# Feature products of the first block: head and tail of the tokens in one 512-column product, its two halves added by ScalarE and VectorE

## The chip, the cores and the metric

The kernel runs on one core of a Trainium2 chip. The metric is the device time of one execution in microseconds (us), all times below are of this kind.

## The reference

A first block of two layers on 256 tokens of 2048 features, then a second block (modulated norm, banded attention, a two-level mixture of 32 experts). The change is in the first block. Cut to it:

```python
for l in range(DEPTH):                                   # DEPTH = 2
    h = _rms_norm(x, norm_g[l])
    proj = jnp.einsum('bsd,dn->bsn', h, w_in[l])         # 2048 x about 7000
    (a_q, a_k, a_v, a_f, a_gate, b_cq, b_ckv, b_krope, b_gate,
     c_q, c_k, c_v, c_gate) = jnp.split(proj, IN_OFFSETS, axis=-1)
    ...
    a_out = _fox_attention(a_q, a_k, a_v, cum_logf) * silu(a_gate)        # 6 heads
    ...
    b_out = _mla_attention(q_nope, q_rope, k_nope, k_rope, b_v) * silu(b_gate)   # 6 heads
    ...
    c_out = _rms_norm(_diff_attention(...), diff_subln_g[l]) * ... * silu(c_gate)  # 4 heads
    x = x + jnp.einsum('bsm,md->bsd', concat(a_out, b_out, c_out), w_out[l])
```

## The kernel before

All products in fp32 are made of fp32r parts: each operand is split into a head (rounded) and a tail (what is left), and a product is head x head + head x tail + tail x head, three matmuls that add up in one bank of PSUM. The helper `three` issues them (L1022 to L1024).

The weights of the first block come as 73 pieces per layer, 128 partitions x 2048 numbers each, in the order of `layer_schedule`: 16 token pieces and one feature piece kr, then for each of six A heads the feature pieces aq, ak, ag (query, key, gate), four low-rank pieces, six gates bg, for each of four C heads cq, ck, cg, and 16 output pieces. SyncE's queue loads pieces, and in between 64 ada pieces per layer (weights for the second block), into a ring `raw` of five. ScalarE writes a piece's head into `w_head` in two halves (L834), VectorE its tail into `w_tail` (L1232); both rings have three slots. At step g the two engines split piece g + 2. A feature piece on TensorE is 16 steps of k (2048 features by 128), with the weights as the stationary operand and 256 tokens as the moving one; the result, 128 features x 256 tokens, fills half a bank. One of four banks is taken in turn. TensorE adds one to `full`, and VectorE brings the bank out times `rrow`, the tokens' inverse norms: L1308 for q (with the scale), L1311 for k, and L1326 for a gate, which then is bounded below in L1327. It then adds one to `free`.

All engines follow one list of steps, `all_steps`, each in its own order of instructions. Between the pieces stand the steps of the heads, sorted by `in_turn`: first score, then gated, then gate, then turn, value and others, then ada, soft. In a score TensorE multiplies q by k (L1171; A adds the decay in L1176), VectorE adds the mask and takes the maximum (L1423 to L1431, "shifted"), ScalarE takes the exponentials (L984, L986). In gate VectorE does L1326 and L1327 into the single buffer `gate_raw`, ScalarE then the sigmoid (L955 to L957), and in gated (L1334), a piece later, VectorE multiplies the two. In soft VectorE scales the probabilities (L1437 to L1440), which TensorE transposes in turn (L1184) after the next piece. In value TensorE multiplies by v (L1193, L1195), and VectorE brings this out (L1469, for C L1462 and the square L1464, whose sum over features TensorE makes in L1201). In ada VectorE multiplies an ada piece and sums it (L1347). L1485 and L1013 split the mixed heads for the output pieces.

The second block has semaphores, tallies and a list of its own and starts when the first is done.

Of the kernel before, what the change touches and what calls it, by code (L numbers as in the profile page):

```python
# [21 lines left out]
F32R = mybir.dt.float32r  # L22
I32 = mybir.dt.int32
ALU = mybir.AluOpType
# [33 lines left out]
class Tally:  # L58

    def __init__(self):
        self.order = {}

    def add(self, sem, event, it=0):
        table = self.order.setdefault(sem, {})
        assert (event, it) not in table, (sem, event, it)
        table[event, it] = len(table) + 1

    def at(self, sem, event, it=0, each=1):  # L70

# [410 lines left out]
def first_block(nc, whole, ctx, d, x, ssq_x, ssq_g, c0, mod):  # L482
# [40 lines left out]
    for l, s in flat:  # L523
        kind = s[0]
        if kind == "squares":
            for t in range(TT):
                tally.add("squared", (s[1], t), l)
            if s[1] == 3 and l < DEPTH:
                tally.add("rstd", "x", l)
        elif kind == "gained":  # L530
            for t in range(TT):
                tally.add("gained", (s[1], t), l)
                tally.add("squared", ("gained", s[1], t), l)
        elif kind == "x_diag":
            tally.add("diag", "x", l)
        elif kind == "split_x":
            tally.add("h_head", s[1], l)
            tally.add("h_tail", s[1], l)
        elif kind == "low_stats":
            tally.add("rstd", "low", l)  # L540
            tally.add("diag", "low", l)
        elif kind == "low_norm":
            for j in range(3):
                tally.add("low_head", j, l)
                tally.add("low_tail", j, l)
        elif kind == "mixed":
            tally.add("m_head", s[1], l)
            tally.add("m_tail", s[1], l)
        elif kind == "forget":
            tally.add("f_abs", 0, l)  # L550
            tally.add("f_ln", 0, l)
        elif kind == "cumsum":
            tally.add("cum", 0, l)
        elif kind == "cum_head":
            tally.add("cum_head", 0, l)
        elif kind == "cum_tail":
            tally.add("decay", 0, l)
        elif kind == "rope":
            tally.add("roped", s[1], l)
        elif kind == "score":  # L560
            tally.add("shifted", s[1:], l)
            tally.add("exped", s[1:], l)
            if s[1] != "C" or s[3] == 1:
                tally.add("probs", s[1:3], l)
        elif kind == "subnorm":
            tally.add("osq", s[1], l)
            tally.add("orstd", s[1], l)
            tally.add("c_mixed", s[1], l)
        elif kind == "piece" and s[2] == "feat" and s[3] in ("ag", "bg", "cg"):
            tally.add("gate", s[2:], l)  # L570
            tally.add("sigmoid", s[2:], l)
    at = tally.at
# [7 lines left out]
    def sb(name, shape, dt=F32):  # L580
        return ctx.enter_context(nc.sbuf_tensor(f"s1_{name}", shape, dt))
# [2 lines left out]
    w_head = sb("w_head", [P, SPLITS, CHUNK_ELEMS], F32R)  # L584
    w_tail = sb("w_tail", [P, SPLITS, CHUNK_ELEMS], F32R)
    c_row = sb("c_row", [P, CHUNK_ELEMS])
    h_head = sb("h_head", [P, KT, T], F32R)
    h_tail = sb("h_tail", [P, KT, T], F32R)
    mixed = sb("mixed", [P, KT, T])
    par = sb("par", [P, DEPTH, N_PAR])  # L590
    rrow = sb("rrow", [P, T])
# [93 lines left out]
    def free_sem(event, l):  # L685
        return sem[f"free{bank_of[event, l]}"]
# [135 lines left out]
    def _(act):  # L822
# [15 lines left out]
        if True:  # L838
            chain = Chain(act, sem["act_chain"])
            for l, s in flat:  # L840
# [52 lines left out]
                elif kind == "piece":  # L893
# [5 lines left out]
                    if what == "tok" and s[4] == 3:  # L899
                        b = s[3]  # L900
                        for t in range(TT):
# [22 lines left out]
                            else:  # L924
                                act.wait_ge(sem["rel_out"], 16)
                                ins = act.activation(v_c[:, t, :], ps[:, :], ACT.Copy, scale=r)
                            ins.then_inc(free_sem(ev, l), 1)
                    elif what == "low":
                        for u in range(4):
                            ev = ("low", s[3], u)  # L930
# [16 lines left out]
                elif kind == "gate":  # L947

                    ev = s[1]
                    n = gate_no[ev] - 3  # L950
                    if n >= 0 or l:
                        gate_used(act, *before(gates, n, l))
# [65 lines left out]
    def _(pe):  # L1018

        def three(out, head, tail, m_head, m_tail, first, last):  # L1020

            pe.matmul(out, head, m_head, start=first, stop=False, skip_group_check=True)  # L1022
            pe.matmul(out, head, m_tail, start=False, stop=False, skip_group_check=True)  # L1023
            return pe.matmul(out, tail, m_head, start=False, stop=last, skip_group_check=True)  # L1024

        pe.wait_ge(sem["x_in0"], 32)
        if True:
            for l, s in flat:
# [27 lines left out]
                elif kind == "piece":  # L1056
# [158 lines left out]
    def _(dve):  # L1215
# [20 lines left out]
        if True:  # L1236
            for l, s in flat:
# [54 lines left out]
                elif kind == "piece":  # L1292
# [5 lines left out]
                    if what == "feat" and s[3] in ("aq", "ak", "cq", "ck", "kr"):  # L1298
                        ev = s[2:]
                        name, h = s[3], s[4]  # L1300
                        ps = full(dve, ev, l)
                        if name == "kr":
                            freed(dve, ("x_rows",), l)
                            out = kr[:, :]
                        else:
                            out = qk[:, h % 2, 0 if name[1] == "q" else 1, :]
                        if name[1] == "q":
# [10 lines left out]
                elif kind == "gate":  # L1318
# [4 lines left out]
                        last, l_last = before(gates, gate_no[ev] - 1, l)  # L1323
                        dve.wait_ge(sem["gate"], at("gate", last, l_last))
                    ps = full(dve, ev, l)
                    chain.link(dve.tensor_tensor(gate_raw[:, :], ps[:, 0:T], rrow[:, :], ALU.mult))  # L1326
                    dve.tensor_scalar(gate_raw[:, :], gate_raw[:, :], -43.0, None, ALU.max)\  # L1327
                       .then_inc(free_sem(ev, l), 1)
                elif kind == "gated":
# [156 lines left out]
                                      ALU.subtract).then_inc(sem["m_tail"], 1)  # L1486
            x_done(dve, DEPTH - 1)

# [61 lines left out]
    return late[:, 0:576].rearrange("p (k e) -> p k e", k=KT), late[:, 576:592], late[:, 592:628]  # L1550


def second_attention(nc, whole, ctx, d, x, ssq_all, c0, mod, mod_dram, shared):
# [67 lines left out]
    for s in steps:  # L1621
# [19 lines left out]
    sem = {name: whole.enter_context(nc.semaphore(f"b2_{name}"))  # L1641
           for name in list(tally.order) + ["dve_chain", "pool_chain", "consts", "first_normed", "rel_in", "mod_rows",
                                            "router_in", "router_w", "router_part", "x_squared"]}

# [1152 lines left out]
def build(nc, d, out):  # L2797


    with ExitStack() as ctx:  # L2800
# [5 lines left out]
        mod = ctx.enter_context(nc.sbuf_tensor("mod", [P, 8, KT], F32))  # L2806
        mod_dram = nc.dram_tensor("mod_rows", [8, D], F32, kind="Internal").ap()
        with ExitStack() as part:
            first_block(nc, ctx, part, d, x, ssq_x, ssq_g, c0, mod)
        shared = {name: ctx.enter_context(nc.sbuf_tensor(name, shape, F32))  # L2810
                  for name, shape in (("logit", [P, 2, 64]), ("early", [P, 4 * T]), ("rstd3", [P, TT]),
                                      ("gain3", [P, KT]), ("sconst", [P, 36]))}
        with ExitStack() as part:
            second_attention(nc, ctx, part, d, x, ssq_all, c0, mod, mod_dram, shared)
        with ExitStack() as part:
            experts(nc, ctx, part, d, x, ssq_x, c0, mod, mod_dram, out, shared)
```

## Time and profile before

| | |
|---|---|
| three runs | 2292.45, 2294.72, 2298.57 us, median 2294.72 |
| profiled execution | 2297.24 us, of it 2295.6 us from the first to the last instruction |
| granted TensorE clock, mean | 0.989 of full |
| first block | about 0 to 941 us |
| second block without experts | to about 1300 us |
| experts | to the end |

The span is what the trace shows; the time of an execution has 1.6 us around it here. PE is TensorE, PEld its weight loads, DVE VectorE, ACT ScalarE, SP SyncE. Records of matmuls overlap, so the distance of their starts is what one costs in a row of them.

### The profile page before, as it was taken

The numbers are of one execution on the slowest core, as the hardware profiler recorded it, in microseconds if no ns is written. First come the engines' busy times: TensorE is split into PE (matmuls) and PEld (weight loads), VectorE is DVE, ScalarE is ACT, GpSimd is POOL, SyncE is SP. The second block draws the span as 40 slices with busy tenths as digits, with TensorE's granted clock in tenths as the row PEclk, the third lists the DMA queues.
The fourth block names the chain that finished last, engine by engine and source line by source line (L and its number), as shares of the span: only waits on it lengthen the run. The fifth ranks groups of instructions, "written<-read, shape, count | busy, mean of one in ns | idle before, by whom it ended". The sixth has DMA issues, their size and how long they took to land. (4 is left out here: it accounts for less than half of the span.)

```text
span 2295.6 us, 35407 instructions
## 1 busy us (share of the span) xinstructions
PE 2142.6 (93%) x14337; PEld 1622.9 (71%) x14337; DVE 1379.6 (60%) x2163; ACT 731.3 (32%) x1324; POOL 40.3 (2%) x62
## 2 busy tenths in 40 slices
PE   8999999999999999899999979998888888888896
PEld 6899999888999998788897755554444444444443
DVE  6988889988888899655565453333333333333334
ACT  6544555455445554566555320000000000000001
POOL 0010000000000000110000000000000000000000
PEclk9999999999999999999999989999999999999998
DMA  9988777988887779654344189999999999999996
GB/s 341 364 336 324 278 261 282 359 338 346 328 323 282 259 280 377 238 197 148 136 147 164 39 368 428 429 431 430 429 431 430 433 430 429 430 429 431 430 429 289
DMA packets 72496, 760.64 MB, mean 331 GB/s; under 512 B 8224, under 2 KB 11200, under 8 KB 13888
## 3 DMA queue, kind: packets, MB, share of 16 engines
q1 hardware_dynamic: 72240, 758.31, 82.5%
q8 instruction: 76, 1.25, 0.2%
q10 hardware_dynamic: 144, 0.79, 0.1%
q14 instruction: 36, 0.29, 0.0%
HBM read 756.12 MB, written 2.95 MB: 331 GB/s over the span
## 5 line engine op out<-in xcount | busy, mean ns | idle before, releaser
L1232 DVE TENSOR_TENSOR s_w_tail<-s_raw,s_w_head 128x1024 fp32r<-128x1024 f32 x292 | 345.2, 1223 | 17.8 <-ACT s_w_head L834 17.7
L1022 PE MATMUL b_ps<-s_h_head,s_w_head 128*128 128x256 f32 x1184 | 341.0, 288 | 0.0
L834 ACT ACTIVATE s_w_head<-s_raw 128x1024 fp32r<-128x1024 f32 x292 | 294.4, 1051 | 141.9 <-DMA s_raw<-in_w 90.6
L1023 PE MATMUL b_ps<-s_h_tail,s_w_head 128*128 128x256 f32 x1184 | 334.8, 283 | 0.0
L1024 PE MATMUL b_ps<-s_h_head,s_w_tail 128*128 128x256 f32 x1184 | 334.8, 283 | 0.0
L1347 DVE CUSTOM_DVE_ANT_0 s_raw<-s_raw,s_c_row 128x2048 f32<-128x2048 f32 x128 | 292.3, 2284 | 0.2
L2466 PE MATMUL b_ps<-s_raw,s_window 128*64 128x256 f32 x2048 | 229.3, 382 | 38.8 <-DMA s_raw<-in_w_up 20.7
L2466 PEld LDWEIGHTS b_ps<-s_raw,s_window 128*64 128x64 f32 x2048 | 156.0, 138 | 117.2 <-issue 31.9
L1022 PEld LDWEIGHTS b_ps<-s_h_head,s_w_head 128*128 128x128 f32 x1184 | 226.7, 192 | 4.2 <-issue 3.9
L1023 PEld LDWEIGHTS b_ps<-s_h_tail,s_w_head 128*128 128x128 f32 x1184 | 227.0, 192 | 0.2
L1024 PEld LDWEIGHTS b_ps<-s_h_head,s_w_tail 128*128 128x128 f32 x1184 | 226.8, 192 | 0.0
L2406 ACT ACTIVATE s_hidden<-b_ps 128x256 f32<-128x256 f32 x32 | 12.3, 384 | 596.8 <-PE b_ps L2466 596.8
L2706 DVE TENSOR_TENSOR x_tokens<-b_ps,x_tokens 128x1024 f32<-128x1024 f32 x128 | 147.8, 1217 | 32.5 <-PE b_ps L2506 32.5
L2698 DVE TENSOR_TENSOR s_y<-b_ps,s_gate_row 128x512 f32<-128x512 f32 x64 | 44.3, 692 | 203.0 <-PE b_ps L2490 203.0
L1022 PE MATMUL b_ps<-s_w_head,s_h_head 128*128 128x512 f32 x416 | 164.3, 395 | 0.7 <-DVE s_w_tail L1232 0.7
L1023 PE MATMUL b_ps<-s_w_tail,s_h_head 128*128 128x512 f32 x416 | 163.4, 393 | 0.0
L1024 PE MATMUL b_ps<-s_w_head,s_h_tail 128*128 128x512 f32 x416 | 163.1, 392 | 0.0
L2069 DVE TENSOR_TENSOR s_w_tail<-s_raw,s_w_head 128x1024 fp32r<-128x1024 f32 x104 | 124.8, 1244 | 47.1 <-ACT s_w_head L1794 47.1
L2466 PE MATMUL b_ps<-s_down,s_window 128*64 128x256 f32 x1024 | 114.0, 380 | 19.2 <-DMA s_down<-in_w_up 12.0
L2466 PE MATMUL b_ps<-s_spare,s_window 128*64 128x256 f32 x1024 | 114.0, 380 | 17.0 <-DMA s_spare<-in_w_up 9.8
L2490 PE MATMUL b_ps<-s_raw,s_diag 128*64 128x512 f32 x512 | 113.4, 595 | 8.2 <-ACT s_diag L2412 8.2
L1925 PE MATMUL b_ps<-s_h_head,s_w_head 128*128 128x256 f32 x416 | 119.7, 288 | 0.9 <-ACT s_v L1834 0.9
(356 smaller groups left out, 3393.0 us busy)
## 6 DMA issues: line engine op xcount, KB each, us to landing
s_raw<-in_w SPq DMA_DIRECT2D x198, 1024.0 KB, 5.1
s_raw<-in_w_ada SPq DMA_DIRECT2D x128, 1024.0 KB, 6.3
s_raw<-in_w_gate SPq DMA_DIRECT2D x16, 4096.0 KB, 32.8
s_raw<-in_w_up SPq DMA_DIRECT2D x16, 4096.0 KB, 30.7
s_raw<-in_w_down SPq DMA_DIRECT2D x32, 2048.0 KB, 26.9
s_down<-in_w_down SPq DMA_DIRECT2D x16, 2048.0 KB, 27.5
s_spare<-in_w_gate SPq DMA_DIRECT2D x8, 4096.0 KB, 32.9
s_down<-in_w_gate SPq DMA_DIRECT2D x8, 4096.0 KB, 32.9
```

The source lines that it names most:

```text
L834: act.activation(w_head[:, g % SPLITS, cols], raw[:, ring, cols], ACT.Copy)\
L1022: pe.matmul(out, head, m_head, start=first, stop=False, skip_group_check=True)
L1023: pe.matmul(out, head, m_tail, start=False, stop=False, skip_group_check=True)
L1024: return pe.matmul(out, tail, m_head, start=False, stop=last, skip_group_check=True)
L1232: dve.tensor_tensor(w_tail[:, g % SPLITS, cols], raw[:, slot["w", g], cols], w_head[:, g % SPLITS, cols].bitcast(F32), ALU.subtract)\
L1347: dve.tensor_tensor_reduce(out=raw[:, ring, :], in0=raw[:, ring, :], in1=c_row[:, :], scale=1.0, scalar=0.0, op0=ALU.mult, op1=ALU.add, ac ...
L1925: pe.matmul(out, head, m_head, start=first, stop=False, skip_group_check=True)
L2069: dve.tensor_tensor(w_tail[:, i % SPLITS, cols], raw[:, i % RAW, cols], w_head[:, i % SPLITS, cols].bitcast(F32), ALU.subtract)\
L2466: ins = pe.matmul(psum[64 * h:64 * h + 64, c // 4, 0:T], window[:, 4 * (c % 4) + k, :], wide[c // 4][:, c % 4, k * 512 + h * T:k * 512 + h ...
L2490: ins = pe.matmul(psum[rows_n, 4 + n % 2, :], hidden_t[:, m_ % 2, 64 * (m_ // 2):64 * (m_ // 2) + 64], down_j[:, m_, n * 512:(n + 1) * 512 ...
L2698: dve.tensor_tensor(y[:, b, :], psum[:, 4 + b, :], gate_row[:, b, :], ALU.mult)\
L2706: dve.tensor_tensor(xs, psum[:, bank:bank + 2, :], xs, ALU.add).then_inc(sem["x_added"], 1)
```

## The change

The head and the tail of the normed tokens, `h_head` and `h_tail`, now lie side by side in one tensor `h_both`, so that for each k they are 512 numbers in a row. For the 36 feature pieces per layer other than kr, a step of k is two matmuls in place of three: the weights' head by all 512 columns, which fills the whole bank (head x head in the left half, head x tail in the right), and the weights' tail by the 256 of the tokens' head into the left half. The two halves have to be added. ScalarE copies the right half to where the result will be (`qk` or `gate_raw`) and adds one to a new semaphore `feat_tail`; VectorE waits for it, adds the left half, and then does from SBUF what it did from PSUM. To save semaphores for the new one, the second block goes on with those of the banks and of the ring, from the counts at which the first leaves them.

```diff
-    h_head = sb("h_head", [P, KT, T], F32R)
-    h_tail = sb("h_tail", [P, KT, T], F32R)
+    h_both = sb("h_both", [P, KT, 2, T], F32R)
+    h_head, h_tail = h_both[:, :, 0, :], h_both[:, :, 1, :]
...
+                    elif what == "feat" and s[3] in ("aq", "ak", "cq", "ck"):
+                        ev = s[2:]
+                        name, h = s[3], s[4]
+                        ps = full(act, ev, l)
+                        act.activation(qk[:, h % 2, 0 if name[1] == "q" else 1, :], ps[:, T:2 * T], ACT.Copy)\
+                           .then_inc(sem["feat_tail"], 1)
...
                 elif kind == "gate":
 
                     ev = s[1]
+                    if gate_no[ev] or l:
+                        last, l_last = before(gates, gate_no[ev] - 1, l)
+                        act.wait_ge(sem["gate"], at("gate", last, l_last))
+                    ps = full(act, ev, l)
+                    act.activation(gate_raw[:, :], ps[:, T:2 * T], ACT.Copy).then_inc(sem["feat_tail"], 1)
...
-                            ins = three(ps[:, 0:T], wh[:, k * P:(k + 1) * P], wt[:, k * P:(k + 1) * P],
-                                        h_head[:, k, :], h_tail[:, k, :], k == 0, k == KT - 1)
+                            if s[3] == "kr":
+                                ins = three(ps[:, 0:T], wh[:, k * P:(k + 1) * P], wt[:, k * P:(k + 1) * P],
+                                            h_head[:, k, :], h_tail[:, k, :], k == 0, k == KT - 1)
+                                continue
+                            pe.matmul(ps[:, :], wh[:, k * P:(k + 1) * P], h_both[:, k, :, :].rearrange("p a c -> p (a c)"),
+                                      start=k == 0, stop=False, skip_group_check=True)
+                            ins = pe.matmul(ps[:, 0:T], wt[:, k * P:(k + 1) * P], h_head[:, k, :], start=False,
+                                            stop=k == KT - 1, skip_group_check=True)
...
+                        dve.wait_ge(sem["feat_tail"], at("feat_tail", ev, l))
+                        chain.link(dve.tensor_tensor(out, ps[:, 0:T], out, ALU.add))
                         if name[1] == "q":
-                            dve.scalar_tensor_tensor(out=out, in0=ps[:, 0:T], scalar=(128 if name[0] == "a" else 64) ** -0.5, in1=rrow[:, :], op0=ALU.mult, op1=ALU.mult)\
+                            dve.scalar_tensor_tensor(out=out, in0=out, scalar=(128 if name[0] == "a" else 64) ** -0.5, in1=rrow[:, :], op0=ALU.mult, op1=ALU.mult)\
                                .then_inc(free_sem(ev, l), 1)
                         else:
-                            dve.tensor_tensor(out, ps[:, 0:T], rrow[:, :], ALU.mult).then_inc(free_sem(ev, l), 1)
+                            dve.tensor_tensor(out, out, rrow[:, :], ALU.mult).then_inc(free_sem(ev, l), 1)
...
                     ps = full(dve, ev, l)
-                    chain.link(dve.tensor_tensor(gate_raw[:, :], ps[:, 0:T], rrow[:, :], ALU.mult))
+                    dve.wait_ge(sem["feat_tail"], at("feat_tail", ev, l))
+                    chain.link(dve.tensor_tensor(gate_raw[:, :], ps[:, 0:T], gate_raw[:, :], ALU.add))
+                    chain.link(dve.tensor_tensor(gate_raw[:, :], gate_raw[:, :], rrow[:, :], ALU.mult))
...
-    tally = Tally()
+    tally = Tally(ring_counts)
```

Lines below L560 have other numbers after the change, about 3 to 27 higher. Where ScalarE stands in an A head of the change, from the exponentials of a score (L998, L1000) to the transposed probabilities (L1008):

```order
L998 ACTIVATE s_s_buf,s_stat<-s_s_buf,s_stat 128x128
L1000 ACTIVATE s_s_buf,s_stat<-s_s_buf,s_stat 128x256
L963 ACTIVATE s_gate_raw<-b_ps 128x256
L969 ACTIVATE s_vc_gate<-s_gate_raw 128x256
L970 ACTIVATE s_vc_gate<-s_vc_gate 128x256
L971 ACTIVATE s_vc_gate<-s_vc_gate 128x256
L837 ACTIVATE s_w_head<-s_raw 128x1024 x2
L935 ACTIVATE s_qk<-b_ps 128x256
L1008 ACTIVATE s_p_t<-b_ps 128x384
```

and the same place before:

```order
L984 ACTIVATE s_s_buf,s_stat<-s_s_buf,s_stat 128x128
L986 ACTIVATE s_s_buf,s_stat<-s_s_buf,s_stat 128x256
L955 ACTIVATE s_vc_gate<-s_gate_raw 128x256
L956 ACTIVATE s_vc_gate<-s_vc_gate 128x256
L957 ACTIVATE s_vc_gate<-s_vc_gate 128x256
L834 ACTIVATE s_w_head<-s_raw 128x1024 x2
L994 ACTIVATE s_p_t<-b_ps 128x384
```

Two copies are new: L963 behind the exponentials, and L935 between the head split and the transposed probabilities. VectorE in the same head, from the end of the score to the eviction of aq, before:

```order
L1431 TENSOR_SCALAR s_stat<-s_stat 128x2
L1326 TENSOR_TENSOR s_gate_raw<-b_ps,s_rrow 128x256
L1327 TENSOR_SCALAR s_gate_raw<-s_gate_raw 128x256
L1347 ISA s_raw,mod<-s_raw,s_c_row 128x2048
L1347 ISA mod 128x1
L1437 RECIPROCAL s_stat<-s_stat 128x2
L1439 TENSOR_SCALAR s_s_buf<-s_s_buf,s_stat 128x128
L1440 TENSOR_SCALAR s_s_buf<-s_s_buf,s_stat 128x256
L1232 TENSOR_TENSOR s_w_tail<-s_raw,s_w_head 128x1024 x2
L1308 SCALAR_TENSOR_TENSOR s_qk<-b_ps,s_rrow 128x256
```

and with the change:

```order
L1458 TENSOR_SCALAR s_stat<-s_stat 128x2
L1352 TENSOR_TENSOR s_gate_raw<-b_ps,s_gate_raw 128x256
L1353 TENSOR_TENSOR s_gate_raw<-s_gate_raw,s_rrow 128x256
L1354 TENSOR_SCALAR s_gate_raw<-s_gate_raw 128x256
L1374 ISA s_raw,mod<-s_raw,s_c_row 128x2048
L1374 ISA mod 128x1
L1464 RECIPROCAL s_stat<-s_stat 128x2
L1466 TENSOR_SCALAR s_s_buf<-s_s_buf,s_stat 128x128
L1467 TENSOR_SCALAR s_s_buf<-s_s_buf,s_stat 128x256
L1252 TENSOR_TENSOR s_w_tail<-s_raw,s_w_head 128x1024 x2
L1331 TENSOR_TENSOR s_qk<-b_ps,s_qk 128x256
L1333 SCALAR_TENSOR_TENSOR s_qk<-s_qk,s_rrow 128x256
```

L1352 and L1331 are the added instructions, each behind a wait for ScalarE's copy; nothing else has changed places.

## Rows read from the trace of the kernel before

**Rows 1.** The page: busy time, share and instructions of each engine

```profile
PE 2142.6 (93%) x14337; PEld 1622.9 (71%) x14337; DVE 1379.6 (60%) x2163; ACT 731.3 (32%) x1324; POOL 40.3 (2%) x62
```

**Rows 2.** Groups of TensorE, 60 to 940 us: count, busy, mean, idle before

```profile
L1022 PE MATMUL b_ps<-s_h_head,s_w_head 128*128 128x256 f32 x1184 | 341.0, 288 | 0.0
```

**Rows 3.** Windows (length; PE, PEld, DVE, ACT, POOL busy; clock; DMA): A, C heads

```profile
122.00:238.00 116.00, 116.00 (x933) 112.64 (x932) 96.84 (x149) 49.54 (x77) 5.77 (x4) 1.00 0.89 330
...
313.00:391.00 78.00, 78.00 (x641) 75.81 (x640) 73.23 (x139) 40.63 (x76) 0.00 (x0) 1.00 0.78 290
```

**Rows 4.** Timeline of VectorE over one A head

```profile
198.89 0.06 DVE L1423 MEMSET s_carrier<- 128x1 f32 x1 [1.97 <-PE b_ps L1176]
...
199.61 0.17 DVE L1431 TENSOR_SCALAR s_stat<-s_stat 128x2 f32<-128x2 f32 x1
199.69 0.42 DVE L1326 TENSOR_TENSOR s_gate_raw<-b_ps,s_rrow 128x256 f32<-128x256 f32 x1
200.15 0.29 DVE L1327 TENSOR_SCALAR s_gate_raw<-s_gate_raw 128x256 f32<-128x256 f32 x1
...
211.46 0.42 DVE L1469 TENSOR_TENSOR s_mixed<-b_ps,s_vc_gate 128x256 f32<-128x256 f32 x1 [0.23 <-PE b_ps L1195]
...
218.34 0.06 DVE L1423 MEMSET s_carrier<- 128x1 f32 x1 [1.97 <-PE b_ps L1176]
```

**Rows 5.** Waits of VectorE from 261.4 to 317 us: total, times, longest

```profile
DVE s_carrier L1423 <- PE b_ps L1171: 5.5, 5, 1.3
```

**Rows 6.** Waits of VectorE from 317 to 396 us

```profile
DVE s_carrier L1423 <- PE b_ps L1171: 2.5, 2, 1.5
DVE s_h_tail L1485 <- ACT s_h_head L1013: 1.5, 2, 1.3
```

**Rows 7.** Timeline of TensorE in a feature piece: start, length; three products apart

```profile
300.13 0.28 PE L1022 MATMUL b_ps<-s_h_head,s_w_head 128*128 128x256 f32 x1
...
300.49 0.28 PE L1022 MATMUL b_ps<-s_h_head,s_w_head 128*128 128x256 f32 x1
```

**Rows 8.** Timeline of TensorE in an output piece, three products apart

```profile
449.83 0.39 PE L1022 MATMUL b_ps<-s_w_head,s_h_head 128*128 128x512 f32 x1
...
450.51 0.39 PE L1022 MATMUL b_ps<-s_w_head,s_h_head 128*128 128x512 f32 x1
```

**Rows 9.** Timeline of ScalarE behind the same score

```profile
199.81 0.40 ACT L984 ACTIVATE s_s_buf<-s_s_buf,s_stat 128x128 f32<-128x128 f32 x1 [7.39 <-DVE s_stat L1431]
...
200.71 0.40 ACT L955 ACTIVATE s_vc_gate<-s_gate_raw 128x256 f32<-128x256 f32 x1
```

**Rows 10.** Timeline of ScalarE: a copy-sized activation out of PSUM

```profile
378.11 0.48 ACT L998 ACTIVATE s_o_c<-b_ps,c_sb 128x256 f32<-128x256 f32 x1 [1.05 <-PE b_ps L1201]
```

**Rows 11.** Timeline of both engines in a B piece

```profile
304.31 0.42 DVE L1326 TENSOR_TENSOR s_gate_raw<-b_ps,s_rrow 128x256 f32<-128x256 f32 x1
...
304.78 0.19 ACT L986 ACTIVATION_READ_ACCUMULATOR s_s_buf<-s_s_buf,s_stat 128x1 f32 x1
```

**Rows 12.** Timeline of both engines behind a C head's scores

```profile
372.80 0.42 DVE L1326 TENSOR_TENSOR s_gate_raw<-b_ps,s_rrow 128x256 f32<-128x256 f32 x1
...
373.86 0.40 ACT L955 ACTIVATE s_vc_gate<-s_gate_raw 128x256 f32<-128x256 f32 x1
```

**Rows 13.** Timeline, A head: probabilities ready, TensorE's transpose of them

```profile
222.41 0.35 DVE L1440 TENSOR_SCALAR s_s_buf<-s_s_buf,s_stat 128x256 f32<-128x256 f32 x1
...
223.98 0.49 PE L1184 MATMUL b_ps<-c_sb,s_s_buf 128*128 128x128 f32 x3
```

**Rows 14.** Timeline, C head: the square ready, TensorE's product of it

```profile
395.40 0.43 DVE L1464 TENSOR_TENSOR s_o_c<-s_o_c 128x256 f32<-128x256 f32 x1
...
396.96 0.38 PE L1201 MATMUL b_ps<-s_o_c,c_sb 128*128 128x256 f32 x1
```

**Rows 15.** A drop of the granted clock: window table, TensorE's pause

```profile
1115.00:1120.00 5.00, 4.53 (x13) 3.67 (x14) 0.00 (x0) 0.42 (x1) 0.00 (x0) 0.66 0.44 184
...
1115.47 0.48 PE L2024 MATMUL b_ps<-s_squares,c_sb 128*128 128x256 f32 x1 [2.33 <-ACT s_squares L1884]
```

More of the change, by code:

```diff
@@ L58, with __init__ @@
 class Tally:
-    def __init__(self):
+    def __init__(self, before=None):
         self.order = {}
+        self.before = before or {}
     def add(self, sem, event, it=0):
@@ L67, in add @@
         assert (event, it) not in table, (sem, event, it)
-        table[event, it] = len(table) + 1
+        table[event, it] = self.before.get(sem, 0) + len(table) + 1
     def at(self, sem, event, it=0, each=1):
@@ L568, in first_block @@
             tally.add("c_mixed", s[1], l)
-        elif kind == "piece" and s[2] == "feat" and s[3] in ("ag", "bg", "cg"):
+        if kind == "piece" and s[2] == "feat" and s[3] != "kr":
+            tally.add("feat_tail", s[2:], l)
+        if kind == "piece" and s[2] == "feat" and s[3] in ("ag", "bg", "cg"):
             tally.add("gate", s[2:], l)
@@ L1306, in _ @@
                             out = qk[:, h % 2, 0 if name[1] == "q" else 1, :]
+                        if name == "kr":
+                            dve.tensor_tensor(out, ps[:, 0:T], rrow[:, :], ALU.mult).then_inc(free_sem(ev, l), 1)
+                            continue
+                        dve.wait_ge(sem["feat_tail"], at("feat_tail", ev, l))
+                        chain.link(dve.tensor_tensor(out, ps[:, 0:T], out, ALU.add))
                         if name[1] == "q":
-                            dve.scalar_tensor_tensor(out=out, in0=ps[:, 0:T], scalar=(128 if name[0] == "a" else 64) ** -0.5, in1=rrow[:, :], op0=ALU.mult, op1=ALU.mult)\
+                            dve.scalar_tensor_tensor(out=out, in0=out, scalar=(128 if name[0] == "a" else 64) ** -0.5, in1=rrow[:, :], op0=ALU.mult, op1=ALU.mult)\
                                .then_inc(free_sem(ev, l), 1)
                         else:
-                            dve.tensor_tensor(out, ps[:, 0:T], rrow[:, :], ALU.mult).then_inc(free_sem(ev, l), 1)
+                            dve.tensor_tensor(out, out, rrow[:, :], ALU.mult).then_inc(free_sem(ev, l), 1)
                     if what == "out" and s[4] == 3:
@@ L1487, in _ @@
             x_done(dve, DEPTH - 1)
+    passed_on = [f"full{b}" for b in range(8)] + [f"raw{n}" for n in range(RAW)]
+    return {name: sem[name] for name in passed_on}, {name: len(tally.order[name]) for name in passed_on}
 HEADS_2 = 16
@@ L1550, in router_views, with second_attention @@
     return late[:, 0:576].rearrange("p (k e) -> p k e", k=KT), late[:, 576:592], late[:, 592:628]
-def second_attention(nc, whole, ctx, d, x, ssq_all, c0, mod, mod_dram, shared):
+def second_attention(nc, whole, ctx, d, x, ssq_all, c0, mod, mod_dram, shared, ring_sems, ring_counts):
     steps = second_schedule()
-    tally = Tally()
+    tally = Tally(ring_counts)
     pieces = [s for s in steps if s[0] == "piece"]
@@ L1640, in second_attention @@
     at = tally.at
-    sem = {name: whole.enter_context(nc.semaphore(f"b2_{name}"))
+    sem = {name: ring_sems[name] if name in ring_sems else whole.enter_context(nc.semaphore(f"b2_{name}"))
            for name in list(tally.order) + ["dve_chain", "pool_chain", "consts", "first_normed", "rel_in", "mod_rows",
@@ L2808, in build @@
         with ExitStack() as part:
-            first_block(nc, ctx, part, d, x, ssq_x, ssq_g, c0, mod)
+            ring_sems, ring_counts = first_block(nc, ctx, part, d, x, ssq_x, ssq_g, c0, mod)
         shared = {name: ctx.enter_context(nc.sbuf_tensor(name, shape, F32))
@@ L2813, in build @@
         with ExitStack() as part:
-            second_attention(nc, ctx, part, d, x, ssq_all, c0, mod, mod_dram, shared)
+            second_attention(nc, ctx, part, d, x, ssq_all, c0, mod, mod_dram, shared, ring_sems, ring_counts)
         with ExitStack() as part:
```

## Prediction

> **What bounds the kernel now.** I read the views from coarse to fine. The page gives TensorE 93% of the span of 2295.6 us, more than any other engine [rows 1]. A busy TensorE is not yet a bound, because its records overlap, so the next view is the groups of matmuls with the idle time ahead of them, cut to 60 to 940 us, which is nearly the whole first block: the first of each three feature products, which is where a wait for a new piece would stand, shows 0.0 us idle before its 1184 records [rows 2]. In the first block TensorE waits for nobody. The table by stage says who comes next: in the A-head stage (122 to 238 us) VectorE is busy 96.84 of 116 us, in the C stage (313 to 391) 73.23 of 78 [rows 3]. So VectorE has 17% and 6% to spare, and ScalarE is idle about half the time. The change touches nothing behind the first block.
>
> The question is then whether VectorE's spare time is larger than what the change takes from it. The spare time is in few places. In each A head VectorE idles 1.97 us before the score, waiting for TensorE [rows 4]; between 261.4 and 317 us such waits sum to 5.5 us, between 317 and 396 us to 4.0 us [rows 5, 6]. The second layer repeats this pattern.
>
> **TensorE's share of the change.** 72 feature pieces (36 per layer, all but the shared kr piece) have 16 steps each. Three products of 256 columns start 0.36 us apart, 0.120 us each [rows 7]. Three of 512 columns start 0.68 us apart, 0.227 us each [rows 8]. A step was 0.360 and becomes 0.227 + 0.120 = 0.347 us: 0.013 us less, 0.21 us a piece, 15.4 us over 72 pieces. The columns streamed are the same, 768; what goes away is one start per step. The same two rows give that start: 0.240 for twice 256 columns against 0.227 for once 512. The Trainium skill, "TensorE: Matmul & The Clock Gate", Back-to-back issue gap, puts the gap of matmuls at the columns over 2.4 GHz plus about 2.5 ns, so that a removed start would be worth 2.5 ns and the whole gain 2.9 us. The rows here disagree with it for these fp32r products. By the page's figure only the gain of each layer's first head (0.64 us, below) would shrink, to 0.12, and the forecast would rise by about 1 us.
>
> **VectorE's share: work.** Every eviction of a feature piece gets one instruction more: first bank plus tail copy, then what was there. The nearest row is the gate's first product, 128x256 out of PSUM, after which its chained successor starts 0.46 us later (199.69 to 200.15) [rows 4]. I take 0.46 us for the added one; the second, now from SBUF, I leave at the old length. The bounds are its own length, 0.42 us, and 0.5.
>
> **VectorE's share: a new wait.** This is the larger term. For a gate piece both engines come to the score first: VectorE writes the shifted scores and goes on to the gate at once, 199.61 to 199.69. ScalarE begins its exponentials only when that is done (7.39 us idle before 199.81) and is free at 200.71, where its gate activation starts today [rows 9]. The tail copy stands behind those exponentials in ScalarE's order. A copy of 128x256 out of PSUM takes 0.48 us [rows 10], and from one engine's end to the other's start I count 0.03 us, as from 199.78 to 199.81 here. VectorE therefore can't start its add before about 200.71 + 0.48 + 0.03 = 201.22 instead of 199.69: 1.53 us standing. With the added instruction everything behind it on VectorE is late by 2.0 us: the ada product, the softmax scaling, the tail split. In a B piece VectorE does the previous gate's product in between, gets to the gate at 304.31, and ScalarE's last read of the exponentials is at 304.78, so the copy could start at about 304.88, in the middle of that read, and be seen at 305.39: 1.08 us standing, 1.54 with the instruction [rows 11]. In a C head there are two scores ahead: VectorE is there at 372.80, ScalarE free at 373.86, so 1.57 us, 2.03 in all [rows 12]. For the q and k pieces I expect no wait: ScalarE copies when the piece ends, and VectorE comes to them after the split of a tail, which it reaches late already. ScalarE's 72 copies, 34 us, lie in its idle time; they also hold up its head splits by up to 3 us (it now waits for the end of ak before it splits the next one), which VectorE, being later still, should not see.
>
> **The ledger of one layer.** "Late" is against the old time of the same instruction.
> A heads: VectorE's cycle was 19.45 us (198.89 to 218.34), with 1.97 + 0.23 idle [rows 4]. Three added instructions and one wait make it 19.45 - 2.20 + 1.38 + 1.53 = 20.16, 0.71 more. TensorE's own cycle would be 19.45 - 0.64 = 18.81, so VectorE decides. The first head has no score yet and gains 0.64; five cycles cost 3.55: the sixth score is 2.9 late. Its probabilities are 4.9 late; TensorE took them 1.2 us after they were there (222.41 + 0.35, against 223.98) [rows 13], so TensorE goes on 3.7 late.
> B heads: the low-rank pieces leave VectorE time to draw level. Then six pieces with 1.54 each, 9.2, less the 5.5 us of idle [rows 5]: at the last probabilities VectorE is 3.7 + 3.7 = 7.4 late.
> C heads: eight q and k evictions (3.7 us) and four gates of 2.03 (8.1), less 4.0 of idle [rows 6]: 15.2 late when the third head's square is written (395.40 + 0.43). TensorE took this 1.1 us later, at 396.96 [rows 14]. So TensorE goes into the output pieces 14.1 us late, and nothing there gives time back, as it already runs without a gap.
> The second layer has the same order and starts with VectorE level again. Two layers: 28.2 us. The profiled execution took 2297.24 us, 1.6 us more than its span; it would be 2325.4. It lies 2.5 us above the median of 2294.72, and against that median I predict 2323 us.
>
> What is queued behind the standing VectorE: the 2.3 us ada product, the softmax scaling that TensorE's transpose needs, and the split of the piece after next. Of these only the scaling binds in the A stage, and the sum of all binds from B on. SyncE's queue waits for tail splits and ada products and so issues later by the same amount; with VectorE slower the DMA share of 0.89 and 0.78 in these stages [rows 3] falls, so no DMA term is added.
>
> **The rivals.**
> 1. VectorE's spare time hides it all. Then only TensorE's 15.4 us show: 2279 us. For it: TensorE has no waits now, ScalarE is half idle. Against it: 0.71 us a head are missing in A with no buffer that could hold them, since the probabilities have 1.2 us of room. It decides if the copy does not have to stand behind the exponentials: A's cycle would be 18.63, under TensorE's 18.81. 8%.
> 2. The lateness is real but smaller: the added instructions cost 0.42 (72 x 0.04 = 2.9 us less), and ScalarE needs half the time I count before its copy is seen (0.75 us less at the nine gates of A and C per layer that count, 13.5 us): 2307. 12%. A balance of gain and loss within 0.3%, 2288 to 2302: 4%.
> 3. TensorE's clock drops. In the old trace the granted clock is 0.66 from 1115 to 1120, that is at the lower level, 1.2 GHz, for part of it; TensorE had stood 2.33 us before 1115.47 [rows 15]. The new waits make pauses of 1 us per A head and 2 us after B. A drop like that one, 5 x 0.34 = 1.7 us lost, behind every of the 12 A heads would add up to 20 us: 2343. It decides if the pause before a piece, half as long at A as that one, is enough for such a drop. The page "TensorE: Matmul & The Clock Gate" of the Trainium skill, HAM oscillation, describes the loss of the full clock from repeated waits. No row of the old trace shows it for pauses of 1 us. 8%.
> 4. The range of my own forecast, VectorE as the bound with 20 to 35 us lost: 68%.
>
> **How the numbers follow.** Predicted 2323. Rival 2's 2307 and, above, rival 3's 2343 bound 8 in 10; with a little room below I give 2304 to 2342. A change under 0.3%, 7 us, can't be told from none. Faster 8% (rival 1), same 4%, slower 88%.
>
> **What will show it.** The feature products in pairs 0.347 us apart. VectorE idle about 1.5 us before the gate's add in A and C, 1.1 in B, released by ScalarE's copy. The idle of 1.97 us before the score gone. The cycle of an A head at 20.2 us, of a C head near 21. TensorE, without a wait in the old trace, waiting for VectorE's probabilities in A (about 1 us a head), after B, and in C for the squares or tails. The prediction is wrong if ScalarE's copy is there before VectorE has finished the shift, if TensorE's waits appear elsewhere, or if the pair takes less than 0.34 us.

## The result and the profile after

The changed kernel took 2325.87 us (median of 4 runs), the kernel before, beside it, 2294.51: a ratio of 1.0132 with an interval of 1.0119 to 1.0144, 31 us or 1.3% slower. The profiled execution took 2325.84 us, with a span of 2324.2 us against 2295.6.

The page of the changed kernel has the busy time by engine and the two feature products. TensorE is as busy as before [rows 1], in a longer span: what was added to the span is time in which it stood or ran at the lower clock, less what the pair saved.

```profile
PE 2142.0 (92%) x13185; PEld 1562.6 (67%) x13185; DVE 1409.4 (61%) x2235; ACT 749.7 (32%) x1396; POOL 40.1 (2%) x62
...
L1108 PE MATMUL b_ps<-s_h_both,s_w_head 128*128 128x512 f32 x1152 | 414.9, 403 | 0.0
L1110 PE MATMUL b_ps<-s_h_both,s_w_tail 128*128 128x256 f32 x1152 | 322.9, 280 | 0.0
```

The waits of the changed kernel from 60 to 970 us (total, times, longest). The old kernel's TensorE had none before 940 us.

```profile
PE b_ps L1204 <- DVE s_s_buf L1467: 9.8, 12, 1.9
PE b_ps L1221 <- DVE s_o_c L1491: 9.0, 4, 3.3
PE b_ps L1191 <- issue: 4.8, 3, 1.7
PE b_ps L1036 <- DVE s_w_tail L1252: 2.8, 2, 1.4
PE b_ps L1213 <- ACT s_p_t L1008: 2.7, 2, 1.4
...
DVE s_gate_raw L1352 <- ACT s_gate_raw L963: 42.5, 32, 1.5
...
DVE s_qk L1331 <- ACT s_qk L935: 9.0, 4, 2.4
```

VectorE waits at all 32 gates for ScalarE's copy. TensorE then waits 29.1 us in all: 9.8 for probabilities (ten times in A, five a layer, 8.9 us, and once a layer at the end of B), 2.8 and 2.7 at the ends of the A and the B stage, 9.0 for the squares of C, and 4.8 before three scores of C (L1191). The 9.0 us ahead of L1331 are no new standing: in the old kernel VectorE stood there too, at the same four pieces, 9.6 us for TensorE.

The timeline of the changed kernel (start, length, engine, line, idle before). First one A head on VectorE and ScalarE, which answers to [rows 4, 9]; then the gates of a B piece and of a C head; then what TensorE waits for.

```profile
197.96 0.06 DVE L1450 MEMSET s_carrier<- 128x1 f32 x1 [0.23 <-PE b_ps L1196]
...
198.68 0.17 DVE L1458 TENSOR_SCALAR s_stat<-s_stat 128x2 f32<-128x2 f32 x1
199.68 0.19 ACT L1000 ACTIVATION_READ_ACCUMULATOR s_s_buf<-s_s_buf,s_stat 128x1 f32 x1
199.77 0.36 ACT L963 ACTIVATE s_gate_raw<-b_ps 128x256 f32<-128x256 f32 x1
200.26 0.42 DVE L1352 TENSOR_TENSOR s_gate_raw<-b_ps,s_gate_raw 128x256 f32<-128x256 f32 x1 [1.42 <-ACT s_gate_raw L963]
200.72 0.42 DVE L1353 TENSOR_TENSOR s_gate_raw<-s_gate_raw,s_rrow 128x256 f32<-128x256 f32 x1
...
217.86 0.06 DVE L1450 MEMSET s_carrier<- 128x1 f32 x1
...
308.33 0.42 DVE L1352 TENSOR_TENSOR s_gate_raw<-b_ps,s_gate_raw 128x256 f32<-128x256 f32 x1 [1.08 <-ACT s_gate_raw L963]
...
361.83 0.42 DVE L1352 TENSOR_TENSOR s_gate_raw<-b_ps,s_gate_raw 128x256 f32<-128x256 f32 x1 [1.47 <-ACT s_gate_raw L963]
...
224.30 0.55 PE L1204 MATMUL b_ps<-c_sb,s_s_buf 128*128 128x128 f32 x3 [0.73 <-DVE s_s_buf L1467]
...
353.85 0.42 DVE L1336 TENSOR_TENSOR s_qk<-s_qk,s_rrow 128x256 f32<-128x256 f32 x1
354.37 1.01 PE L1191 MATMUL b_ps<-s_qk 64*128 64x128 f32 x8 [1.67 <-issue]
...
407.71 0.80 PE L1221 MATMUL b_ps<-s_o_c,c_sb 128*128 128x256 f32 x1 [3.17 <-DVE s_o_c L1491]
...
838.91 0.70 PE L1221 MATMUL b_ps<-s_o_c,c_sb 128*128 128x256 f32 x2 [2.00 <-DVE s_o_c L1491]
...
882.74 0.70 PE L1221 MATMUL b_ps<-s_o_c,c_sb 128*128 128x256 f32 x2 [3.28 <-DVE s_o_c L1491]
```

VectorE ends the shift at 198.85 and stands until 200.26. ScalarE begins its copy only when the second exponential has been read, at 199.77. The idle time ahead of the score, 1.97 us before [rows 4], is 0.23 and then nothing. This A head takes 19.90 us (197.96 to 217.86), the old one 19.45; the others of this layer take 19.7 to 20.1. The wait "on issue" at 354.37 is one for the key: its eviction on VectorE ends at 354.27, behind the tail split that VectorE reached late.

The window tables of the changed kernel (columns as in [rows 3]): the A heads, the C stage, and four short stretches inside the C heads and behind them.

```profile
122.00:242.00 120.00, 115.18 (x664) 97.99 (x663) 105.48 (x174) 53.10 (x98) 6.05 (x4) 1.00 0.84 314
322.00:402.00 80.00, 76.36 (x430) 64.28 (x428) 74.34 (x142) 40.02 (x78) 0.00 (x0) 0.98 0.74 272
...
354.00:359.00 5.00, 4.63 (x20) 3.81 (x21) 5.00 (x9) 0.00 (x0) 0.00 (x0) 0.66 0.99 395
406.00:414.00 8.00, 6.29 (x16) 4.99 (x17) 7.76 (x17) 5.81 (x9) 0.00 (x0) 0.57 0.37 131
840.00:844.00 4.00, 4.00 (x15) 3.42 (x14) 3.86 (x10) 3.97 (x7) 0.00 (x0) 0.57 0.44 143
...
878.00:886.00 8.00, 4.72 (x21) 3.60 (x20) 6.25 (x21) 6.05 (x17) 0.00 (x0) 1.00 0.35 122
```

In the first three short ones the granted clock is at the lower level, 1.2 GHz, for part of the time: 0.34 x 5 + 0.43 x 8 + 0.43 x 4 = 6.9 us lost at most. In the fourth, around the longest pause of all, it stays full. The old kernel had one such fall in the first block, at 80 to 90 us (granted 0.83, 1.7 us), which this execution of the new one did not have, so some 5 us are from the clock. 29.1 of waits and 5 of clock, less the 7.4 that the pair gives (measured below), make 27; the span grew by 28.6. The sum is rough: a matmul's record lasts 0.28 us where the next starts 0.12 us later, so each of the 23 waits is some 0.16 us longer than its record, which is 4 us more.

### The profile page after: what moved, and what is told of

It reads as the page before. It is cut to its first block and busy times, and to the rows that moved or that the text cites. A ratio compares the mean times of both kernels' runs of the same rounds, so it can differ in the third digit from the quotient of the medians.

```text
span 2324.2 us, 33319 instructions
## 1 busy us (share of the span) xinstructions
PE 2142.0 (92%) x13185; PEld 1562.6 (67%) x13185; DVE 1409.4 (61%) x2235; ACT 749.7 (32%) x1396; POOL 40.1 (2%) x62
## 5 line engine op out<-in xcount | busy, mean ns | idle before, releaser
L1108 PE MATMUL b_ps<-s_h_both,s_w_head 128*128 128x512 f32 x1152 | 414.9, 403 | 0.0
L1110 PE MATMUL b_ps<-s_h_both,s_w_tail 128*128 128x256 f32 x1152 | 322.9, 280 | 0.0
L1108 PEld LDWEIGHTS b_ps<-s_h_both,s_w_head 128*128 128x128 f32 x1152 | 217.7, 189 | 53.8 <-issue 2.5
L1110 PEld LDWEIGHTS b_ps<-s_h_both,s_w_tail 128*128 128x128 f32 x1152 | 218.4, 190 | 0.2
L1036 PE MATMUL b_ps<-s_w_head,s_h_both 128*128 128x512 f32 x416 | 163.2, 392 | 0.7 <-DVE s_w_tail L1252 0.7
L1037 PE MATMUL b_ps<-s_w_tail,s_h_both 128*128 128x512 f32 x416 | 162.2, 390 | 0.0
L1038 PE MATMUL b_ps<-s_w_head,s_h_both 128*128 128x512 f32 x416 | 162.0, 389 | 0.0
L2496 PE MATMUL b_ps<-s_down,s_window 128*64 128x256 f32 x1024 | 114.0, 380 | 19.7 <-DMA s_down<-in_w_up 12.4
L2718 DVE TENSOR_TENSOR s_hidden<-b_ps,s_hidden 128x256 f32<-128x256 f32 x32 | 13.6, 425 | 176.7 <-PE b_ps L2496 176.7
L1955 PE MATMUL b_ps<-s_h_head,s_w_head 128*128 128x256 f32 x416 | 119.7, 288 | 0.9 <-ACT s_v L1864 0.9
L2536 PE MATMUL b_ps<-s_y,s_weigh_t 64*128 64x512 f32 x512 | 118.5, 602 | 0.0
```

The lines of the kernel that those rows point to most:

```text
L1108: pe.matmul(ps[:, :], wh[:, k * P:(k + 1) * P], h_both[:, k, :, :].rearrange("p a c -> p (a c)"), start=k == 0, stop=False, skip_group_che ...
L1110: ins = pe.matmul(ps[:, 0:T], wt[:, k * P:(k + 1) * P], h_head[:, k, :], start=False, stop=k == KT - 1, skip_group_check=True)
L2496: ins = pe.matmul(psum[64 * h:64 * h + 64, c // 4, 0:T], window[:, 4 * (c % 4) + k, :], wide[c // 4][:, c % 4, k * 512 + h * T:k * 512 + h ...
L2536: ins = pe.matmul(psum[:, PART_BANKS[t][n], :], weigh_t[rows_n, t * P:(t + 1) * P], y[rows_n, n % 2, :], start=True, stop=True)
```

## The experiments

Medians are shown with the ratio to the kernel before, run beside it (2294.1 to 2295.4 us). An experiment's line numbers are its own.

**1. The copy ahead of the exponentials.** ScalarE's lines for the gate's copy move from the step "gate" to the step of the gate's piece:

```diff
+                    elif what == "feat" and s[3] in ("ag", "bg", "cg"):
+                        ...                      # waits for the last gate and for full
+                        act.activation(gate_raw[:, :], ps[:, T:2 * T], ACT.Copy).then_inc(sem["feat_tail"], 1)
                 elif kind == "gate":
-                    act.activation(gate_raw[:, :], ps[:, T:2 * T], ACT.Copy).then_inc(sem["feat_tail"], 1)
```

> The changed kernel with one edit: ScalarE copies the gate's half in the step of the gate's own piece, ahead of the exponentials that it now queues behind, instead of in the gate's step. Theory (the loss is VectorE standing at each gate for that copy, 1.4 us in A and C, 1.1 in B): the wait goes from 42.5 us over 32 gates to under 10, an A head's cycle goes back from 20.0 us to at most the 19.45 of before, C keeps its two added instructions a piece and stays up to 1 us a head above before; in all 2288 to 2302 us. Rival (the added VectorE instructions cost by themselves, the wait only fills time that was idle anyway): 2315 us or more. Rival (the loss is the TensorE clock that fell in three new places, at most 7 us of 31): not under 2315 either, unless the falls go too.

Measured: 2292.26 us, 0.9987 [0.9977, 0.9996]. This single move gives back 33.6 us, more than the whole loss. In the timeline of this version, over the same A head, VectorE goes from the shift to the add without a stop, since the copy was made from 195.63 to 196.01, in time that ScalarE had idle; the cycle is 18.95 us (196.70 to 215.65):

```profile
195.63 0.38 ACT L943 ACTIVATE s_gate_raw<-b_ps 128x256 f32<-128x256 f32 x1 [3.98 <-PE b_ps L1112]
196.70 0.06 DVE L1452 MEMSET s_carrier<- 128x1 f32 x1 [0.56 <-PE b_ps L1198]
...
197.41 0.17 DVE L1460 TENSOR_SCALAR s_stat<-s_stat 128x2 f32<-128x2 f32 x1
197.52 0.42 DVE L1354 TENSOR_TENSOR s_gate_raw<-b_ps,s_gate_raw 128x256 f32<-128x256 f32 x1
...
215.65 0.06 DVE L1452 MEMSET s_carrier<- 128x1 f32 x1 [0.56 <-PE b_ps L1198]
```

Its waits from 60 to 970 us: VectorE's at the gates are down from 42.5 to 5.5 us, TensorE's in A and B are gone, and some 4.5 us are left in C, for keys and squares (and one of 1.3 us at 893 us, behind C's heads):

```profile
PE b_ps L1193 <- issue: 2.9, 2, 1.5
PE b_ps L1223 <- DVE s_o_c L1493: 1.6, 4, 0.5
...
DVE s_gate_raw L1354 <- ACT s_gate_raw L943: 5.5, 10, 0.6
```

**2. The change for queries and keys alone.** Gates with three products and the old eviction.

```diff
-                            if s[3] == "kr":
+                            if s[3] in ("kr", "ag", "bg", "cg"):
```

> The pair of products and the side by side columns for the pieces aq, ak, cq and ck alone (40 of 72 pieces, 40 added VectorE instructions); the gates as before the change, with three products and no copy by ScalarE. Theory (waiting at the gates' copy is most of the loss): 2288 to 2300 us, that is within 6 us of the kernel before. Rival (added VectorE work by itself): over half of the 31 us remains, 2310 or more.

Measured, within the theory's range: 2289.91 us, 0.9982 [0.9971, 0.9992]. 40 of the 72 added instructions are in it, and it is faster than before. So the queries and keys by themselves are not where the loss is. Beside the gates' wait they are not free: the changed kernel is 8 us slower than the next version, which leaves them as they were.

**3. The change for the gates alone.** The reverse, `if s[3] in ("kr", "aq", "ak", "cq", "ck")`.

> The pair of products and ScalarE's copy for the 32 gates alone; the pieces for queries and keys as before the change. Theory (the wait at the gates is most of the loss): 2308 to 2322 us. Rival (added VectorE work by itself, 32 of 72 instructions): 2300 to 2308.

Measured: 2317.44 us, 1.0101 [1.0079, 1.0122]: 23 us slower, as the theory had it, with 32 instructions added and the same 42.4 us of waits at the gates.

**4. The pair without its price.** The two products, with the evictions of before. Nobody adds the right half, so head x tail is left out of the features.

> The two products of the changed kernel with the evictions of before: nobody reads the half that holds the weights' head times the tokens' tail, so the features leave that term out. It measures what TensorE alone gives. By the traces' rows (a k step of 0.347 to 0.353 us in place of 0.360, 16 steps a piece, 72 pieces) 7 to 15 us less than before, 2279 to 2287, less if VectorE's cycle in C takes part of it. By the Trainium skill's gap between back to back products the three and the pair would differ by 2.9 us in all, 2291.

Measured: 2286.74 us, 0.9964 [0.995, 0.9979]: 7.4 us faster, 5 to 11 by the interval, at the low end of what the rows had promised. The timeline of this version shows a part of why. In 45 of its 72 feature pieces the steps begin 0.353 us apart (132.47 to 133.53 for three), not 0.347, most of it since the first product takes 0.236 us there on average; in the other 27 they are 0.347 apart, with 0.231 for the first product. By these starts TensorE saves about 10.4 us, which lies in the interval, too; where the median's other 3 us are stays open.

```profile
132.47 0.40 PE L1095 MATMUL b_ps<-s_h_both,s_w_head 128*128 128x512 f32 x1
132.71 0.28 PE L1097 MATMUL b_ps<-s_h_both,s_w_tail 128*128 128x256 f32 x1
132.83 0.40 PE L1095 MATMUL b_ps<-s_h_both,s_w_head 128*128 128x512 f32 x1
...
133.53 0.40 PE L1095 MATMUL b_ps<-s_h_both,s_w_head 128*128 128x512 f32 x1
```

**5. The added work without the wait.** The old kernel, with an add out of PSUM ahead of each of the 72 evictions.

```diff
+                            chain.link(dve.tensor_tensor(out, ps[:, 0:T], rrow[:, :], ALU.add))
...
+                    chain.link(dve.tensor_tensor(gate_raw[:, :], ps[:, 0:T], rrow[:, :], ALU.add))
```

> The kernel before the change, with one more VectorE instruction at each of the 72 feature evictions (an add that reads the bank, overwritten by the next instruction), and no copy by ScalarE to stand for; TensorE as before. Theory (wait and added work draw on the same slack of VectorE, which neither uses up by itself): 2296 to 2304 us. Rival (the added work is the loss by itself, the wait falls into idle time): 2315 or more. Rival (the wait alone is the loss): within 1 us of before.

Measured: 2296.50 us, 1.0005 [0.9995, 1.0014]. 72 instructions of 0.46 us, 33 us of VectorE's time, cost 1 us, which is not clear of nothing. In the timeline the A head keeps its cycle of 19.45 us:

```profile
195.49 0.06 DVE L1425 MEMSET s_carrier<- 128x1 f32 x1 [1.10 <-PE b_ps L1176]
...
214.94 0.06 DVE L1425 MEMSET s_carrier<- 128x1 f32 x1 [1.10 <-PE b_ps L1176]
```

**6. The wait without the added work.** Three products, old evictions. ScalarE makes a copy of the gate's product behind its exponentials, and VectorE waits for it and then overwrites it.

```diff
+                    act.activation(gate_raw[:, :], ps[:, 0:T], ACT.Copy).then_inc(sem["feat_tail"], 1)
...
+                    dve.wait_ge(sem["feat_tail"], at("feat_tail", ev, l))
                     chain.link(dve.tensor_tensor(gate_raw[:, :], ps[:, 0:T], rrow[:, :], ALU.mult))
```

> Three products everywhere and the gates evicted as before the change, but ScalarE first copies the gate's product into the buffer behind its exponentials, and VectorE waits for that copy (then overwrites it); no added VectorE instruction, no gain on TensorE. Theory (wait and added work draw on the same slack): 2296 to 2308 us. Rival (the wait alone is the loss, about 31 us and what TensorE gains): 2320 or more.

Measured: 2303.63 us, 1.0037 [1.0022, 1.0052], 8 us. VectorE stands at the gates for 42.8 us, as in the changed kernel, but TensorE waits only 5.8 us by its records, and the A head takes 19.85 us, with 1.36 us of idle time still ahead of VectorE's score. Timeline:

```profile
198.39 0.06 DVE L1438 MEMSET s_carrier<- 128x1 f32 x1 [1.36 <-PE b_ps L1190]
...
204.38 0.55 PE L1198 MATMUL b_ps<-c_sb,s_s_buf 128*128 128x128 f32 x3 [0.19 <-DVE s_s_buf L1455]
...
218.24 0.06 DVE L1438 MEMSET s_carrier<- 128x1 f32 x1 [1.36 <-PE b_ps L1190]
```

**7. Both, with three products.** The changed kernel's copies, waits and evictions in full, and `three` for every piece. ScalarE's copies take the left half times zero.

> The changed kernel's copies, waits and VectorE instructions in full, but three products a k step as before; ScalarE's copies take the product times zero, so that the sum is what it was. It is added work and wait together without TensorE's gain, which apart cost 1 and 8 us. Theory (they draw on one slack, and cost far more together): 2326 to 2334 us, that of the changed kernel or up to the 7.6 us more that the pair gives where TensorE sets the pace. Rival (they only add up, and the changed kernel loses something else, in the pair itself or in the shape of the h buffer): 2304 to 2310.

Measured: 2331.56 us, 1.0161 [1.0144, 1.0178]. Apart, work and wait cost 1 and 8 us; together 37. (Experiment 7 has ScalarE's 40 copies for q and k as well, which neither of the two others has.) The cycle of the A head in its timeline is 20.31 us:

```profile
199.92 0.06 DVE L1450 MEMSET s_carrier<- 128x1 f32 x1 [0.43 <-PE b_ps L1196]
...
220.23 0.06 DVE L1450 MEMSET s_carrier<- 128x1 f32 x1 [0.43 <-PE b_ps L1196]
```

Three cycles give the law of the A head. The wait alone adds 0.40 us (19.85), work alone nothing (19.45), both 0.86 (20.31). Both less the wait alone is 0.46, one instruction: the one between the shift and the softmax scaling. So there was 1.42 - 0.40 = 1.02 us of room in the path score, gate, ada, scaling, transpose; 0.46 fits in it, 1.42 does not, and once the wait has used it up each added instruction in this path counts in full. That leaves nothing of this cycle for the q and k copies to explain. In C, where the two layers of experiment 7 lose about 20 us (late keys and up to 5 us of clock among it), no run separates the added instructions for q and k from their copies.

**8 and 9. Where it arises.** The early copy for A's and B's gates only, with C's 8 behind the exponentials, and the reverse.

> The changed kernel with ScalarE's copy moved ahead of the exponentials for the gates of A and B (24), and left behind them for C's 8. Theory (C has the least room, and what A and B lose is handed on into it): 2300 to 2310 us, over a third of the 34 us between this change and its version with the early copy everywhere. Rival (A's and B's waits are nearly all of it): under 2298.

> The reverse: the copy early for C's 8 gates, behind the exponentials for the 24 of A and B. Theory (A's heads take 20.0 us where 19.45 were, B adds its part, lateness goes on into C): 2302 to 2316 us. Rival (the loss arises in C alone): under 2298.

Measured: with C's late 2307.02 us, 1.0047 [1.0028, 1.0066]; with A's and B's late 2309.65, 1.0061 [1.0044, 1.0078]. Against the early copy everywhere (0.9987) the first costs 0.60%, the second 0.74%, and both together, which is the changed kernel, 1.45%, so that they nearly add up (1.34). C's 8 gates cost 14 us, 1.7 us each; the 24 of A and B cost 17, 0.7 each. Of C's 14, up to 6.8 us are three falls of the clock in the heads and output pieces of C, which the early copy has not. TensorE's waits from 60 to 970 us, in the version with C's late:

```profile
PE b_ps L1229 <- DVE s_o_c L1499: 8.9, 4, 3.3
PE b_ps L1199 <- issue: 4.3, 3, 1.7
```

and in the version with A's and B's late:

```profile
PE b_ps L1212 <- DVE s_s_buf L1475: 9.2, 12, 1.4
PE b_ps L1199 <- issue: 4.2, 4, 1.5
```

**10 and 11. A version that beats both.** The early copy, and C as before the change, in whole or for its gates alone:

```diff
-                            if s[3] == "kr":
+                            if s[3] in ("kr", "cg", "cq", "ck"):      # 10: C as before;  11: ("kr", "cg")
```

> The version with ScalarE's early copy, but the 24 pieces of C (cq, ck, cg) as before the change: three products, one eviction, no copy; the pair in A and B alone. In the version with the early copy the 5 us of TensorE's waits that were left all stood in C, for the tail splits, scores and values. Theory (added work costs only where VectorE's cycle is as long as TensorE's, in C): those waits go, 2286 to 2290 us. Rival (the added work costs everywhere): 2291 or more, since fewer pieces have TensorE's gain.

> As the run with the pair in A and B alone, but the pair for cq and ck too; only C's gates as before the change. Theory: 2285 to 2289 us, if VectorE's cycle in C has room for two added instructions a head and a half but not for the gates'; rival: above the version without them, by up to 3 us.

Measured: 10 took 2291.13 us, 0.9981 [0.9971, 0.999]; 11 took 2286.52 (four runs, from 2284.89 to 2290.98), 0.9954 [0.9937, 0.997], 0.46% faster than before and the best of all versions that keep every term. For 10 the median is the rival's number, by 0.1 us. Its mechanism isn't: TensorE's waits in the first block are down to 0.2 us, and 48 of 72 pieces with the pair are worth 4.9 us by experiment 4, 4.3 measured; my forecast had left too little for that smaller number of pieces. In 11, TensorE waits 1.9 us for two scores of C, and the pair for cq and ck is worth having all the same. The two intervals meet at 0.997, so that 11 is the faster one is likely, not certain. Its 8.9 us by the medians are more than 64 pieces give by experiment 4 (6.6); the interval holds both.

## Why the prediction was right, and where only its sum was

The predicted time was 2323 us, and 2325.87 was measured. By its steps:

**TensorE's pair: mis-sized.** I had 0.347 us a step and 15.4 us in all. In the changed kernel the steps took 0.353 in 38 pieces and 0.347 in 32, and the gain is 7.4 us where nothing hides it (experiment 4). The formula of the Trainium skill's "TensorE: Matmul & The Clock Gate", Back-to-back issue gap, would give 2.9 us; the interval of 5 to 11 us excludes it and also my 15.4. By that formula one 256-column product takes about 0.109 us, and the rows show 0.120. The section gives it for an isolated product and says that a stream with weight loads, as it runs here, is spaced otherwise, which my prediction left out.

**The added work: right in length, 0.46 us** (200.26 to 200.72).

**The new wait: right.** I had 1.53, 1.08 and 1.57 us in A, B and C, and measured were 1.42, 1.08 and 1.47; ScalarE's copy took 0.36 us and not 0.48, the row that I sized it by. Experiment 1 shows that it is the cause. That q and k cost no wait was right where it mattered: the four waits of 9.0 us in all are at the first head of each layer, where the old VectorE stood 9.6 us, and experiment 2 with all of them is faster than before. Not foreseen was that the key comes late to C's scores.

**The A head's ledger: the right size from the wrong account.** I took VectorE's cycle as the bound, 19.45 - 2.20 + 1.38 + 1.53 = 20.16. It took 19.90, but with three products, where the pair gives nothing, 20.31, and VectorE still had 0.43 us idle in each cycle. So VectorE's idle time was not the room. The room was that of the path through both engines, 1.02 us (I read 1.2 at the probabilities, [rows 13], and used it once, at the end of the stage, not in each head). My account would also have said that the wait alone, 1.42, fits into the 2.20 idle; experiment 6 says that it doesn't. That my figure came near is in part luck: in the changed kernel the pair shortens TensorE's part, VectorE's idle time is nearly gone as well (0.23 us and less), and the two accounts meet. Since TensorE sets the other part of this path, the pair's gain counts in every A head, which I had given to the first only.

**B and C: right in sum.** The third head's square was used at 396.96 before [rows 14] and at 407.71 now, 10.75 us later, in a layer whose A heads began 3.1 us earlier (118.83 against 121.93), so 13.85 us were lost on the way; I had 14.1. Up to 1.7 of the 13.85 are the fall of the clock at 355 us, which my sum had not, so the waits gave some 12. That nothing behind it gives time back was right; the fall at 406 us took more, and by TensorE's starts the first layer lost 16.6 us (118.83 to 593.86 against 121.93 to 580.34) and the second 14.0.

**The clock: a rival that came true in part, elsewhere.** I gave 8% to falls behind the 12 pauses of A. There were none there, with pauses of 0.6 to 0.8 us, one of 1.1 and one of 1.9, and the version with A's and B's copies late had none beyond the old kernel's one. But in C and behind it three came, at or behind pauses of 1.67, 3.17 and 2.00 us. They cost about 5 us more than the old kernel's fall, and the pair gave 5.7 us in this kernel (experiment 7 less the changed one) where my ledger had 1.3. These two errors cancel; the good fit of 2323 is partly due to that.

**Faster and smaller cases.** Rival 1, that VectorE's spare time hides all, was wrong for this kernel, but the point from which I let it decide, the copy not standing behind the exponentials, is what experiment 1 made: there A's cycle was 18.95 (I had 18.81). That version is 0.13% faster and not 0.7%, since C has no room for the added instructions and the pair gives half of what I had, or two thirds by its starts.

## What to carry to other kernels

When an engine is to do a small thing for another one, look at what stands ahead of it in its own order: the same copies of 0.36 us cost 34 us more behind the exponentials than ahead of them. Room is a property of a path and not of an engine: read it at the hand-over (how long was the result there before it was taken, each time round), and expect two costs that fit in it singly (1 and 8 us here) to cost far more together (37). Apply a change piece by piece where stages have different room; here the best version has the pair in all pieces but the gates of C.

## What the runs showed of the hardware

The pair of a 512- and a 256-column product, each with its own weights, takes 0.347 or 0.353 us. Each feature piece has one of the two from its second step to its last (32 and 38 pieces of the changed kernel, 27 and 45 of experiment 4), and what selects one is open.

TensorE's clock fell to its lower level at or behind pauses of 1.67, 2.00 and 3.17 us in the changed kernel. It did not fall behind one of 1.68 (829.40) or the longest, 3.28 (882.74), nor behind the waits for probabilities: one of 1.91, one of 1.10, the rest 0.9 us or less. In the first block of the thirteen traces, from 60 us on, there are 18 pauses of TensorE from 1.6 to 3.3 us. Ten falls go with them, begun within the pause or at most 1.4 us behind it, and none with a shorter pause. So a fall went with about every other such pause, and what decides stays open.

In the old kernel the clock fell once in the first block, at 85 us, behind eight products of 32 rows, with TensorE busy for 10.00 of 10 us:

```profile
82.09 2.84 PE L1034 MATMUL b_ps<-s_s_buf,s_rb 32*128 32x384 f32 x8
...
80.00:90.00 10.00, 10.00 (x34) 6.93 (x33) 9.94 (x12) 4.28 (x6) 0.00 (x0) 0.83 0.98 346
```

This fall stands in eight of the thirteen traces and not in the other five, though all run the same steps there. So a pause is neither needed nor enough. In the first block the clock lost 6.8 us in the changed kernel, 5.1 in experiment 7 and 8.5 in 8, all with C's copies late and two instructions per eviction; it lost at most 3.4 in all others.
